# Two sandwich norms per sub-layer done in two token parts, between the last three and the first three weight tiles on either side

## The chip, the cores and the metric

The kernel runs on one NeuronCore of a Trainium2 chip. The metric is the device time of one execution in microseconds (us). The kernel before takes 1851.71 us (median of 3 runs, 1851.44 to 1854.57).

## The reference

Two layers over 512 latent tokens and 256 context tokens, with 1024 channels. What matters here is what stands between the big matrix products:

```python
for l in range(DEPTH):                              # DEPTH = 2
    u   = modulate(rms_norm(x, g_pre_mix[l]), sh1, sc1) @ w_in[l]      # latent tokens
    uc  = modulate(rms_norm(h_ctx, g_pre_mix[l]), csh1, csc1) @ w_in[l] # context tokens
    ...                                             # four head groups -> concatenated
    mix = jnp.concatenate([...], axis=-1) @ w_out[l]
    x = x + gt1 * rms_norm(mix, g_post_mix[l])
    ffn = swiglu(modulate(rms_norm(x, g_pre_ffn[l]), sh2, sc2), w_ffn_in[l], w_ffn_out[l])
    x = x + gt2 * rms_norm(ffn, g_post_ffn[l])
    if l < DEPTH - 1:
        ...                                         # the same two steps for h_ctx
```

`rms_norm` takes the mean of squares over the 1024 channels of a token. A norm after a product (post norm) therefore needs every output tile of the product, and the norm ahead of the next product (pre norm) needs all of the updated x.

## The kernel before, in words

**Layout.** Channels lie on the 128 partitions in 8 chunks, tokens on the free axis. Layer 0 works on 768 tokens (512 latent, then 256 context), layer 1 after its projections on the 512 latent ones. All matrix products are `L808`: a weight tile of 128 output channels is split into a high and a low part, and for each of its k chunks (8, or 6 in the last FFN group) there are three passes (high by high, high by low, low by high). A pass over 768 tokens is two matmuls of 384 columns, one over 512 tokens a single matmul of 512.

**The weight stream.** 196 tiles of 512 KB are read in order into a ring of 3 slots (`raw`, `w_hi`, `w_lo`). SyncE issues the load of tile k when the product of tile k-3 is done: `stream` waits on the semaphore `blk_done`. ScalarE then makes the high part (`L570`, `split_hi`) and VectorE the low part (`L1154`, `split_lo`), each at a place fixed in the engine's own program; so every engine runs its list in the order written.

**Between two groups of products** all is in one piece over all tokens. I call these places boundaries: B0 (output projection to FFN, layer 0, 768 tokens), B1 (FFN of layer 0 to the projections of layer 1, 768 tokens), B2 (output projection to FFN, layer 1, 512 tokens) and B3 (the end, 512 tokens, post norm and output only). At each one: the last tile is copied (ScalarE, `L579`) or added (VectorE, `L1181`) into `f_t`; GpSimd has summed the squares of tiles 0 to 6 (`L491`, `L493`); ScalarE squares the last tile (`L713`); TensorE sums over partitions with a matrix of ones (`L871`, float32); ScalarE makes the inverse root in two activations (`L708`, `L709`, `inverse_root`); VectorE scales and adds to x chunk by chunk (`post_norm`, `L1248`, `L1252`). Behind it ScalarE squares each chunk of x (`L702`), TensorE sums (`L859`), the root again, and then `pre_norm` makes the next product's input chunk by chunk: VectorE `tmp` (`L1226`), ScalarE `h_hi` (`L723`), VectorE `h_lo` (`L1233`). The first two tiles of the next group are multiplied side by side (`side_by_side`: chunk k into both banks as soon as it is there), and the third one after them.

**Names of tiles below.** At a boundary the eight output tiles before it are 0 to 7, and the tiles after it are 8, 9, 10, 11 and so on.

Of the kernel before, what the change touches and what calls it, by code (L numbers as in the profile page):

```python
# [20 lines left out]
F32 = mybir.dt.float32  # L21
# [4 lines left out]
D = 1024  # L26
# [48 lines left out]
HALF = TOK // 2  # L75

# [73 lines left out]
def hybrid_kernel(nc, xT, cvec, wstream, adaT, badaT, gT, rpb, wf, sink, lbT, hgT, dftL, dftC, dftD, rotm,  # L150
                  rope, swamask, namask, lvmask, sqc, out):
    with ExitStack() as ctx:
# [148 lines left out]
        x_upd, pn_m = sem("x_updated"), sem("post_norm_scaled")  # L301
        mix_done = sem("mixer_done")
# [104 lines left out]

        STEPS = [steps_after(l) for l in range(DEPTH)]
# [6 lines left out]
        def _(sp):  # L415
# [49 lines left out]
            for c in range(0, NC, 2):  # L465
                sp.wait_ge(x_upd, 2 * DEPTH * NC - NC + c + 2)
                sp.dma_start(outT[:, c:c + 2], x[:, c:c + 2, 0:LAT]).then_inc(s_out, 16)
            sp.wait_ge(s_out, 16 * NC // 2)
# [3 lines left out]
        def _(pool):  # L472
# [12 lines left out]

            def squares(g0, b0, n, T):

                for b in range(b0, min(b0 + n, N_OUT - 1)):
                    pool.wait_ge(bank_free[b % 2], g0 + b // 2 + 2)
                    f = f_t[:, b, 0:T]  # L490
                    link(pool.tensor_tensor(sq[:, 1 if b == 0 else 0, 0:T], f, f, ALU.mult))  # L491
                    if b:
                        link(pool.tensor_tensor(sq[:, 1, 0:T], sq[:, 1, 0:T], sq[:, 0, 0:T], ALU.add))  # L493
                    if b == N_OUT - 2:
                        pool.sem_inc(sq_sum, 1)
# [13 lines left out]
            for l in range(DEPTH):  # L509
# [38 lines left out]
                if l == 0:  # L548
                    ada_loads(11, 1)
                    squares(tp["wout"], 0, N_OUT, T)  # L550
                    ada_loads(12, 28)
                else:
                    squares(tp["wout"], 0, N_OUT, T)
                squares(tp["out", len(FFN_CHUNKS) - 1], 0, N_OUT, T)


        @block.scalar
        def _(act):
# [14 lines left out]
            def copy_phase(g0, n, dst, b0, T):  # L573

                for b in range(2 * n):
# [6 lines left out]
            def project(l, b):  # L582
# [5 lines left out]
                act.activation(as_product(u_t[:, blk, 0:T], T), product_of(ps[b % 2], T),  # L588
                               ACT.Silu if blk >= QD else ACT.Copy).then_inc(bank_free[b % 2], 1)

            def projections(l):
                g0 = 2 * TP[l]["proj"]
                for b in range(N_ALONE):
                    split_hi(g0 + b + 2)
# [82 lines left out]
            def splits_only(g0, n):  # L677

                for b in range(2 * n):
                    split_hi(2 * g0 + b + 2)  # L680

            def ffn_in(g0, n, T):
                for i in range(n):
                    k = 2 * (g0 + i)
                    split_hi(k + 2)
                    act.wait_ge(blk_done, k + 1)
                    act.wait_ge(bank_free[1], i + (g0 + 1))
                    act.activation(as_product(tmp[:, 0, 0:T], T), product_of(ps[0], T), ACT.Silu)\
# [22 lines left out]
            def late_mean_square(T):  # L711

                act.activation(lnms[:, 0:T], f_t[:, NC - 1, 0:T], ACT.Square).then_inc(sq_ready, 1)  # L713
                nsq[0] += 1
# [978 lines left out]
```

## Time and profile before

| | |
|---|---|
| median of 3 runs | 1851.71 us |
| profiled execution | 1851.98 us, of which the span from the first to the last instruction is 1850.2 us |
| chain that ended last, by engine | TensorE 85%, VectorE 9%, DMA 3%, ScalarE 2%, issue 1% |
| mean granted TensorE clock | 0.974 of full |
| TensorE busy | 1704.0 us (92% of the span) |
| VectorE, ScalarE, GpSimd busy | 980.6, 596.2, 149.1 us |

A busy TensorE is not one at its peak, since matmuls overlap in the records; the distance from one start to the next is what a matmul costs. "Idle before, releaser" is time in which the engine waited, and what ended the wait.

### The profile page before, as it was taken

The numbers are of one execution on the slowest core, as the hardware profiler recorded it, in microseconds if no ns is written. First come the engines' busy times: TensorE is split into PE (matmuls) and PEld (weight loads), VectorE is DVE, ScalarE is ACT, GpSimd is POOL, SyncE is SP. The second block draws the span as 40 slices with busy tenths as digits, with TensorE's granted clock in tenths as the row PEclk, the third lists the DMA queues.
The fourth block names the chain that finished last, engine by engine and source line by source line (L and its number), as shares of the span: only waits on it lengthen the run. The fifth ranks groups of instructions, "written<-read, shape, count | busy, mean of one in ns | idle before, by whom it ended". The sixth has DMA issues, their size and how long they took to land.

```text
span 1850.2 us, 24632 instructions
## 1 busy us (share of the span) xinstructions
PE 1704.0 (92%) x10460; PEld 1501.7 (81%) x10460; DVE 980.6 (53%) x1603; ACT 596.2 (32%) x796; POOL 149.1 (8%) x186
## 2 busy tenths in 40 slices
PE   2699998999799999999999979898899899999996
PEld 1699987769599999999999959796667587887874
DVE  7987536865566544555554372653762632233334
ACT  2334433732332222221122143542462422332231
POOL 1010001004100000000000400000103000000003
PEclk9899999999899999999999989999999899999998
DMA  8261124132133334333432202113402132232222
GB/s 335 88 204 48 47 63 105 50 114 84 54 103 116 124 125 135 116 126 125 128 113 91 69 23 69 58 47 83 112 34 69 46 102 91 91 102 91 91 92 102
DMA packets 80638, 178.84 MB, mean 97 GB/s; under 512 B 38912, under 2 KB 39424, under 8 KB 80272
## 3 DMA queue, kind: packets, MB, share of 16 engines
q1 hardware_dynamic: 66864, 122.70, 21.7%
q0 software_dynamic: 13664, 54.56, 8.6%
q8 instruction: 83, 1.36, 0.3%
q14 instruction: 27, 0.22, 0.0%
HBM read 175.14 MB, written 2.10 MB: 96 GB/s over the span
## 4 chain that ended last, share of the span: by engine, by line
PE 85%; DVE 9%; DMA 3%; ACT 2%; issue 1%; SPq 0%; DVEq 0%; ACTq 0%
PE psum L808 73%; PE psum L969 2%; PE psum L980 2%; PE psum L1003 2%; DMA ada_0a<-in_adaT 1%; DVE f_t L1248 1%; PE psum L1034 1%; DVE x L1252 1%; PE psum L859 1%; DVE tmp L1226 1%; PE psum L891 1%; DVE psum L1545 1%; DVE w_lo L1154 1%; DVE psum L1166 1%; DVE s_sb L1324 1%
## 5 line engine op out<-in xcount | busy, mean ns | idle before, releaser
L808 PE MATMUL psum<-h_hi,w_hi 128*128 128x384 f32 (+1 forms) x1872 | 560.4, 359 | 32.1 <-DVE h_lo L1233 27.3
L808 PE MATMUL psum<-h_lo,w_hi 128*128 128x384 f32 (+1 forms) x1872 | 547.5, 352 | 0.0
L808 PE MATMUL psum<-h_hi,w_lo 128*128 128x384 f32 (+1 forms) x1872 | 547.2, 352 | 0.0
L1154 DVE TENSOR_TENSOR w_lo<-raw,w_hi 128x1024 fp32r<-128x1024 f32 x194 | 241.2, 1243 | 352.2 <-ACT w_hi L570 350.9
L808 PEld LDWEIGHTS psum<-h_hi,w_hi 128*128 128x128 f32 x1872 | 342.7, 190 | 61.5 <-issue 34.7
L570 ACT ACTIVATE w_hi<-raw 128x1024 fp32r<-128x1024 f32 x194 | 205.6, 1060 | 501.3 <-DMA raw<-in_wstream 501.2
L808 PEld LDWEIGHTS psum<-h_lo,w_hi 128*128 128x128 f32 x1872 | 346.4, 190 | 20.6 <-issue 1.7
L808 PEld LDWEIGHTS psum<-h_hi,w_lo 128*128 128x128 f32 x1872 | 345.6, 190 | 19.9
L1166 DVE CUSTOM_DVE_ANT_0 psum<-ada_w,c_b 128x1024 f32<-128x1024 f32 x160 | 202.2, 1264 | 16.3 <-issue 3.7
L1194 DVE TENSOR_TENSOR tmp<-tmp,psum 128x768 f32<-128x768 f32 (+1 forms) x44 | 36.1, 821 | 263.6 <-PE psum L808 263.6
L808 PE MATMUL psum<-hid_hi,w_hi 128*128 128x384 f32 (+1 forms) x528 | 160.2, 357 | 15.6 <-DVE w_lo L1154 13.2
L808 PE MATMUL psum<-hid_lo,w_hi 128*128 128x384 f32 (+1 forms) x528 | 159.1, 355 | 0.0
L808 PE MATMUL psum<-hid_hi,w_lo 128*128 128x384 f32 (+1 forms) x528 | 159.0, 355 | 0.0
L808 PEld LDWEIGHTS psum<-hid_hi,w_hi 128*128 128x128 f32 x528 | 97.0, 189 | 27.1 <-DVE w_lo L1154 17.3
L808 PEld LDWEIGHTS psum<-hid_hi,w_lo 128*128 128x128 f32 x528 | 97.7, 190 | 7.0
L808 PEld LDWEIGHTS psum<-hid_lo,w_hi 128*128 128x128 f32 x528 | 97.8, 190 | 6.7
L859 PE MATMUL psum<-sq,consts 128*128 128x512 f32 (+1 forms) x112 | 50.0, 604 | 51.8 <-ACT sq L702 51.7
L477 POOL DMA_DIRECT2D ada_w<-in_adaT x78 | 41.3, 530 | 635.7 <-DVE ada_t L1166 635.1
L859 PEld LDWEIGHTS psum<-sq,consts 128*128 128x128 f32 x112 | 23.8, 226 | 77.5 <-issue 50.2
L491 POOL TENSOR_TENSOR sq<-f_t 128x768 f32<-128x768 f32 (+1 forms) x28 | 41.1, 1467 | 537.5 <-DVE f_t L1181 446.6
L692 ACT ACTIVATE hid_hi<-tmp 128x768 fp32r<-128x768 f32 (+1 forms) x44 | 32.5, 739 | 116.8 <-DVE tmp L1194 116.8
L588 ACT ACTIVATE u_t<-psum 128x768 f32<-128x768 f32 (+1 forms) x44 | 33.6, 763 | 100.7 <-PE psum L808 100.4
(168 smaller groups left out, 1453.9 us busy)
## 6 DMA issues: line engine op xcount, KB each, us to landing
raw<-in_wstream SPq DMA_DIRECT2D x196, 512.0 KB, 3.6
ada_w<-in_adaT POOLq DMA_DIRECT2D x80, 512.0 KB, 4.0
ada_0a<-in_adaT SPq DMA_DIRECT2D x6, 1024.0 KB, 14.3
x<-in_xT POOLq DMA_DIRECT2D x4, 1536.0 KB, 10.9
na_r<-in_rpb SPq DMA_DIRECT2D x64, 64.0 KB, 3.4
fn_l<-in_dftL POOLq DMA_DIRECT2D x2, 2048.0 KB, 8.2
ada_0b<-in_adaT SPq DMA_DIRECT2D x2, 1024.0 KB, 19.3
out_xT<-x SPq DMA_DIRECT2D x4, 512.0 KB, 2.8
```

The source lines that it names most:

```text
L477: pool.dma_start(ada_w[:, u], adaT[2 * ADA_ORDER[q] + (2 * ADA_FIRST + u)]).then_inc(ada_ld[u], 16)
L491: link(pool.tensor_tensor(sq[:, 1 if b == 0 else 0, 0:T], f, f, ALU.mult))
L570: act.activation(w_hi[:, k % RING].rearrange("p c n -> p (c n)"), raw[:, k % RING], ACT.Copy)\
L588: act.activation(as_product(u_t[:, blk, 0:T], T), product_of(ps[b % 2], T), ACT.Silu if blk >= QD else ACT.Copy).then_inc(bank_free[b % 2], 1)
L808: mm = pe.matmul(ps[u][:, at:at + hi - lo], w[:, slot, k], r[:, k, lo:hi], start=first, stop=last)
L859: mm = pe.matmul(ps[2][:, lo:hi], ones, sq[:, c % 2, lo:hi], start=c == 0, stop=c == NC - 1)
L969: mm = pe.matmul(dst, q, keys, start=True, stop=True)
L980: mm = pe.transpose(pt_ps[:, n * j + P * c:n * j + P * c + P], s_sb[:, v % 3, j, o:o + P], ident)
L1003: mm = pe.matmul(dst, val, pt_sb[:, v % 2, n * j + P * c:n * j + P * c + P], start=c == 0, stop=c == n // P - 1, skip_group_check=True)
L1154: dve.tensor_tensor(w_lo[:, k % RING].rearrange("p c n -> p (c n)"), raw[:, k % RING], w_hi[:, k % RING].rearrange("p c n -> p (c n)").bit ...
L1166: dve.tensor_tensor_reduce(ps[3][:], ada_w[:, u], c_b[:, v], 1.0, 0.0, ALU.mult, ALU.add, ada_t[:, u, v:v + 1]).then_inc(ada_done, 1)
L1194: dve.tensor_tensor(as_product(tmp[:, 1, 0:T], T), as_product(tmp[:, 0, 0:T], T), product_of(ps[1], T), ALU.mult).then_inc(bank_free[1], 1)
```

## The change

The norms at the four boundaries are done in two token parts. For 768 tokens part 0 is the 256 context tokens and part 1 the 512 latent ones; for 512 tokens the parts are halves of 256. The last three tiles of the product before (5, 6, 7) are multiplied first for part 0 and then for part 1 (`tail`), each into a bank of its own; the first three of the next product (8, 9, 10) first for part 0 and then, chunk by chunk and all three together, for part 1 (`head`). In `head` a part-1 pass over 768 tokens consists of matmuls of 384 and of 128 columns, beside the 256 of part 0. All three of its tiles report `blk_done` only in their last part-1 chunk. The mean squares are put inside these products on TensorE; VectorE and ScalarE get a written order (`norm_by_parts`) in which the weight splits of tiles 8, 9 and 10 stand between pieces of the norms. The gate products of layer 0 (`ada_pair`) start one step later in the FFN, and the output is stored in 8 pieces for 4.

```diff
+TAIL, HEAD = 3, 3
+def norm_parts(T):
+    return ((LAT, TOK, 1, 512), (0, LAT, 0, 0)) if T == TOK else ((0, T // 2, 0, 0), (T // 2, T, 0, 512))
...
+        def tail_bank(j):
+            return ps[(1, 0, 3)[j]]
+        def head_bank(j):
+            return ps[3] if j == HEAD - 1 else ps[j % 2]
...
 @block.gpsimd
+            def tail_squares(g0, T, nb):
+                for p, (lo, hi, _, _) in enumerate(norm_parts(T)):
+                    for j in range(TAIL - 1):
+                        b = N_OUT - TAIL + j
+                        if p == 0:
+                            pool.wait_ge(tail_free, TAIL * nb + j + 1)
+                        else:
+                            pool.wait_ge(bank_free[b % 2], g0 + b // 2 + 2)
+                        square(b, lo, hi)
+                    pool.sem_inc(sq_sum, 1)
...
 @block.scalar, the order at a boundary (norm_by_parts)
+                for j in range(TAIL):
+                    copied(0, j)
+                post_root(0)
+                pre_root(0)
+                copied(1, 0)
+                split_hi(2 * (g0 + N_OUT // 2))
+                normed_hi(0, 0, NC // 2)
+                copied(1, 1)
+                normed_hi(0, NC // 2, NC)
+                split_hi(2 * (g0 + N_OUT // 2) + 1)
+                copied(1, 2)
+                post_root(1)
+                split_hi(2 * (g0 + N_OUT // 2) + 2)
+                pre_root(1)
+                normed_hi(1, 0, NC)
...
 @block.tensor
+            def tail(g0, rhs_hi, rhs_lo, kc, T, nb, pre):
+                parts = norm_parts(T)
+                for p, (lo, hi, _, at0) in enumerate(parts):
+                    for j in range(TAIL):
+                        b = N_OUT - TAIL + j
+                        if p == 0:
+                            pe.wait_ge(w_lo_done, 2 * g0 + b + 1)
...
+                        for k in range(kc):
+                            mm = passes_into(tail_bank(j), 2 * g0 + b, k, rhs_hi, rhs_lo, ((lo, hi, at0),), k == 0, k == kc - 1)
+                            if k == kc - 1:
+                                mm.then_inc(blk_done if p else tail_done, 1)
+                            if p and j == 0 and k == 2:
+                                late_mean_square(parts[0])
+                            if p and j == 1 and pre:
+                                part_mean_square(parts[0], NC * k // kc, NC * (k + 1) // kc)
+            def head(g0, T, nb):
+                for j in range(HEAD):
+                    pe.wait_ge(w_lo_done, 2 * g0 + j + 1)
+                    for k in range(NC):
+                        if j == 0:
+                            pe.wait_ge(hlo_ready, base + k + 1)
+                        passes_into(head_bank(j), 2 * g0 + j, k, h_hi, h_lo, head_pieces(T, 0), k == 0, k == NC - 1)
+                        if j == 0 and k == 3:
+                            late_mean_square(parts[1])
+                part_mean_square(parts[1], 0, NC)
+                for u in range(2):
+                    pe.wait_ge(bank_free[u], g0 + 1)
+                for k in range(NC):
+                    pe.wait_ge(hlo_ready, base + NC + k + 1)
+                    for j in range(HEAD):
+                        mm = passes_into(head_bank(j), 2 * g0 + j, k, h_hi, h_lo, head_pieces(T, 1), k == 0, k == NC - 1)
+                        if k == NC - 1:
+                            mm.then_inc(blk_done, 1)
...
 @block.vector, the order at a boundary (norm_by_parts)
+                for j in range(TAIL):
+                    added(0, j)
+                root()
+                post(0, 0, NC)
+                dve.wait_ge(x_upd, nx[0])
+                added(1, 0)
+                if pre is None:
+                    added(1, 1)
+                    added(1, 2)
+                    root()
+                    post(1, 0, NC)
+                    dve.wait_ge(x_upd, nx[0])
+                    return
+                root()
+                normed(0, 0, NC // 2)
+                split_lo(nxt)
+                added(1, 1)
+                normed(0, NC // 2, NC)
+                split_lo(nxt + 1)
+                added(1, 2)
+                root()
+                post(1, 0, 2)
+                split_lo(nxt + 2)
+                post(1, 2, NC)
+                dve.wait_ge(x_upd, nx[0])
+                root()
+                normed(1, 0, NC)
```

`post(p, c0, c1)` is the post norm and `normed(p, c0, c1)` the pre norm of part p for chunks c0 to c1; `nxt` is tile 8.

## Rows read from the trace of the kernel before

**Rows 1.** Who waited for whom: total us, times, longest.

```profile
PE psum L859 <- ACT sq L702: 51.7, 7, 34.5
PE psum L808 <- DVE h_lo L1233: 27.3, 4, 12.7
```

**Rows 2.** VectorE, SyncE and ScalarE in order of time around B1.

```profile
1069.16 0.95 DVE L1181 TENSOR_TENSOR f_t<-f_t,psum 128x768 f32<-128x768 f32 x1 [0.24 <-PE psum L808]
...
1116.58 18.20 SPq L429 DMA_DIRECT2D raw<-in_wstream  x4
...
1121.19 1.23 DVE L1154 TENSOR_TENSOR w_lo<-raw,w_hi 128x1024 fp32r<-128x1024 f32 x1 [7.13 <-ACT w_hi L570]
...
1126.13 0.81 ACT L588 ACTIVATE u_t<-psum 128x768 f32<-128x768 f32 x1 [2.60 <-PE psum L808]
```

**Rows 3.** ScalarE and VectorE at B0 (two rows), then at B2 (two rows).

```profile
477.21 0.81 ACT L579 ACTIVATE f_t<-psum 128x768 f32<-128x768 f32 x1 [3.73 <-PE psum L808]
...
533.19 0.81 ACT L688 ACTIVATE tmp<-psum 128x768 f32<-128x768 f32 x1 [3.05 <-PE psum L808]
...
1440.23 0.60 ACT L579 ACTIVATE f_t<-psum 128x512 f32<-128x512 f32 x1 [0.87 <-PE psum L808]
...
1484.80 0.69 DVE L1194 TENSOR_TENSOR tmp<-tmp,psum 128x512 f32<-128x512 f32 x1 [3.64 <-PE psum L808]
```

**Rows 4.** The chain: products of 384 and then 512 columns without a wait.

```profile
643.66 200.16 PE psum L808 x1152
...
1563.37 119.98 PE psum L808 x528
```

**Rows 5.** TensorE in order of time: float32 matmuls of 256 and 512 columns.

```profile
379.40 5.63 PE L883 MATMUL psum<-fn_d,u_t 128*128 128x256 f32 x24
385.72 7.13 PE L891 MATMUL psum<-fn_l,fn_ab 128*128 128x512 f32 x16 [0.69 <-ACT fn_ab L778]
```

**Rows 6.** Groups by form: float32 of 128 columns; weight loads of 128 and 64.

```profile
L1082 PE MATMUL psum<-hv,hk 128*128 128x128 f32 x80 | 10.2, 275 | 0.0
...
L808 PEld LDWEIGHTS psum<-h_lo,w_hi 128*128 128x128 f32 x1872 | 346.4, 190 | 20.6 <-issue 1.7
...
L1034 PEld LDWEIGHTS psum<-hq,hs 64*64 64x64 f32 x1120 | 20.0, 137 | 11.1 <-issue 11.1
```

**Rows 7.** The chain at B1: post norm of one chunk, 768 tokens.

```profile
1077.64 1.06 DVE f_t L1248 x2
1078.70 0.87 DVE x L1252
```

**Rows 8.** The chain at B3: last add, root, post norm, 512 tokens.

```profile
1832.72 0.70 DVE f_t L1181
...
1835.34 0.70 ACT lnms L708
...
1836.06 0.64 ACT rstd L709
...
1838.81 0.66 DVE f_t L1248
1839.47 0.60 DVE x L1252
...
1845.79 1.20 DVE x L1252 x2
```

**Rows 9.** ScalarE group by form: h_hi of 256 columns.

```profile
L723 ACT ACTIVATE h_hi<-tmp,col_sh 128x256 fp32r<-128x256 f32 x24 | 11.8, 494 | 0.0
```

**Rows 10.** GpSimd shortly before B2: squares of 512 columns.

```profile
1435.53 1.04 POOL L491 TENSOR_TENSOR sq<-f_t 128x512 f32<-128x512 f32 x1 [3.03 <-ACT f_t L579]
1436.65 1.29 POOL L493 TENSOR_TENSOR sq<-sq 128x512 f32<-128x512 f32 x1
```

**Rows 11.** TensorE at B1, just after the products start again.

```profile
1099.09 0.84 PE L808 MATMUL psum<-h_lo,w_hi 128*128 128x384 f32 x2
1099.73 0.84 PE L808 MATMUL psum<-h_hi,w_lo 128*128 128x384 f32 x2
```

More of the change, by code:

```diff
@@ L802, in passes, with passes_into @@
             def passes(tile, k, rhs_hi, rhs_lo, T, begin, end):
-                u, slot = tile % 2, tile % RING
+                return passes_into(ps[tile % 2], tile, k, rhs_hi, rhs_lo, pieces(T), begin, end)
+            def passes_into(bank, tile, k, rhs_hi, rhs_lo, tokens, begin, end):
+                slot = tile % RING
                 for w, r, first, last in ((w_hi, rhs_hi, begin, False), (w_hi, rhs_lo, False, False),
                                           (w_lo, rhs_hi, False, end)):
-                    for lo, hi, at in pieces(T):
-                        mm = pe.matmul(ps[u][:, at:at + hi - lo], w[:, slot, k], r[:, k, lo:hi], start=first, stop=last)
@@ L1170, in ada_pair, with lo_phase @@
                 dve.tensor_copy(dst, ada_t[:].rearrange("p u v -> p (u v)")).then_inc(ada_copied, 1)
[L1172 removed]
+            def lo_phase(g0, n, ada=(0, 0), add=False, T=TOK, tail=0):
                 for i in range(n):
@@ L1236, in pre_norm, with norm_by_parts, added, root @@
                 dve.wait_ge(hlo_ready, nlo[0])
-            def post_norm(l, gt, g, T):
-                cols(l, gt, col_gg)
-                link(dve.tensor_tensor(col_gg[:], col_gg[:], gain(l, g), ALU.mult))
-                nrs[0] += 1
-                dve.wait_ge(rstd_ready, nrs[0])
-                st = STREAMS[:2 if T == TOK else 1]
-                for c in range(NC + 1):
-                    if c < NC:
-                        for lo, hi, v in st:
+            def norm_by_parts(l, gt, g_post, sh, sc, g_pre, T, g0, nb, add, pre):
+                parts = norm_parts(T)
+                def added(p, j):
+                    if not add:
+                        return
+                    b = N_OUT - TAIL + j
+                    lo, hi, _, at0 = parts[p]
+                    if p == 0:
+                        dve.wait_ge(tail_done, TAIL * nb + j + 1)
+                    else:
+                        dve.wait_ge(blk_done, 2 * g0 + b + 1)
+                    dst = f_t[:, b, lo:hi]
+                    dve.tensor_tensor(dst, dst, tail_bank(j)[:, at0:at0 + hi - lo], ALU.add)\
+                       .then_inc(bank_free[b % 2] if p else tail_free, 1)
+                def root():
+                    nrs[0] += 1
+                    dve.wait_ge(rstd_ready, nrs[0])
+                def post(p, c0, c1):
+                    lo, hi, v, _ = parts[p]
+                    for c in range(c0, c1 + 1):
+                        if c < c1:
@@ new lines, in norm_by_parts @@
+                nxt = 2 * (g0 + N_OUT // 2)
+                cols(l, gt, col_gg)
+                link(dve.tensor_tensor(col_gg[:], col_gg[:], gain(l, g_post), ALU.mult))
+                if pre is not None:
+                    cols(pre, sh, col_sh)
+                    cols(pre, sc, col_sc)
+                    link(dve.scalar_tensor_tensor(col_gs[:], col_sc[:], 1.0, gain(pre, g_pre), ALU.add, ALU.mult))
+                for j in range(TAIL):
+                    added(0, j)
+                root()
```

243 lines of the change are left out of this document (167 added, 76 removed).

## The prediction, on record before the change was run

> **What bounds the kernel now.** I read the page first: TensorE carries 85% of the chain that ended last. The waits then show where it stands still: 51.7 us until ScalarE has squares of x (34.5 of them before the first product, which the change leaves alone) and 27.3 us until VectorE has the first `h_lo` of a product [rows 1]. Both stand at the boundaries. The engines in order of time give what a boundary costs from the start of tile 5 to the start of tile 11, the stretch that the change rewrites. Tile 7 of B1 is done at 1069.13 [rows 2]. A pass of 384 columns takes 200.16 / 1152 = 0.174 us and one of 512 takes 119.98 / 528 = 0.227 us [rows 4], so a tile over 768 tokens takes 8.34 us with 8 chunks and 6.25 us with 6, and over 512 tokens 5.45 and 4.09. Tile 5 of B1 therefore started at 1050.4; tile 10 is done at 1126.1 [rows 2]: **B1 is 75.7 us** long. In the same way **B0** is 533.2 - (477.2 - 25.0) = **81.0** and **B2** is (1484.8 - 5.45) - (1440.2 - 16.35) = **55.5**, since that last row marks tile 11's end [rows 3]. **B3** runs from tile 5 to the end of the span: 1850.2 - (1832.7 - 12.3) = **29.8** [rows 8].
>
> **What stays equal and what is added on TensorE.** Over 768 tokens the tail's parts have the same columns and the same number of matmuls. The head's passes become three matmuls (256, 384, 128) for two. No product (`L808`) of 256 or 128 columns is in the trace. The fixed part of a matmul is 0.174 - 0.160 = 0.014 us, so 256 columns take about 0.12 (0.107 of streaming). For 128 columns there are two bounds: 0.067 by the same sum, and 0.127, the distance of float32 matmuls with 128 columns and a full weight load each (10.2 / 80, [rows 6]). I take 0.12, near the upper one, because the weight load seems to bind: its record is 190 ns for 128 columns of weights and 137 ns for 64 [rows 6], 53 ns more for 64 columns, so a full load occupies some 107 ns, and it is done anew for every matmul. Part 1 of the head then takes 24 x 3 x (0.174 + 0.12) = 21.2 us, part 0 takes 8.6, together 29.8 for 25.0 before: 4.8 us more at B0 and at B1. The Trainium skill ("TensorE: Matmul & The Clock Gate", Back-to-back issue gap) gives columns over 2.4 GHz plus 2.5 ns, about 56 ns for 128 columns; by that B0 and B1 would each be some 4.6 us shorter than I sum. This trace's 14 ns of fixed cost speaks against the 2.5. Over 512 tokens each matmul of 512 becomes two of 256: 0.24 for 0.227.
>
> The mean squares now stand in TensorE's own program. One float32 instruction leaves two records, and records of 256 and 512 columns stand some 0.23 and 0.44 us apart (5.63 / 24 and 7.13 / 16, each a little less because the last one drains), so 256 columns cost 0.46 and 512 cost 0.88 us [rows 5].
>
> **VectorE and ScalarE by parts.** From the two widths [rows 7, 8]: scaling 0.66 for 512 columns and 1.06 - 0.66 = 0.40 for 256; the add 0.60, and by its slope of 0.27 per 256 columns 0.33. So post norm costs 0.73 us a chunk for 256 tokens and 1.26 for 512. A pre-norm chunk of 256 is two scalings and a completion, 0.91; its first `h_lo` needs `tmp`, `h_hi` (0.49 [rows 9]) and `h_lo` in turn, 1.5. Root: 1.36 for 512 [rows 8], 0.96 for 256 (two activations near the 0.49).
>
> **B1, step by step** (t = 0 at the start of tile 5).
> 1. Tile 7's weights are loaded when tile 4 is done, at 0. Load 3.5, `split_hi` 1.1, `split_lo` 1.2: the low part comes 5.84 us after the issue even where nothing is in the way (1121.19 + 1.23 - 1116.58 [rows 2]). Tiles 5 and 6 of part 0 take only 2 x 2.16, so TensorE idles until 6.0; part 0 ends at 8.1.
> 2. Add and square of part 0, its float32 sums behind the third chunk of tile 5 (GpSimd's squares of 256, some 1.4 us a tile from [rows 10], are ready by 10.3), root: 12.4. Post norm 8 x 0.73: 18.3.
> 3. The mean square of part 0 is spread over tile 6, which ends with it at 21.3; root: 22.5. Tile 7 ends at 25.4.
> 4. VectorE could begin the pre norm at 22.5, but ScalarE first does `split_hi` of tile 8 (1.1). Four chunks end at 27.0, and only then comes `split_lo` of tile 8: 28.2. TensorE, done at 25.4, idles 2.9.
> 5. VectorE adds tile 6 (0.6), norms the other four chunks (to 32.7), waits for `split_hi` of tile 9, splits (34.5), adds tile 7 (35.1). Square 0.63: 35.9. TensorE stands in the middle of tile 8, behind the wait for that square, since 29.7: 5.3 us idle there, less one sum.
> 6. Root: 38.4. Post norm of two chunks, `split_lo` of tile 10 (42.1), six more chunks: 49.7. TensorE does the head's part 0 until 45.1 and the eight sums of part 1 until 52.2. Root, `tmp`, `h_hi`, `h_lo`: 56.2, so 4.0 us idle.
> 7. Part 1 of the head: 21.2, to 77.4.
> 8. Tile 11 cannot be loaded before tile 8 is done. Before, tiles 8 and 9 finished together and tile 10 (8.3 us) covered the load. Now all three finish within 1.8 us of the end: 77.4 - 1.8 + 5.84 and some 0.2 of waits is **81.7**, so TensorE idles 4.4.
>
> The serial chain of VectorE and ScalarE has not become shorter; both parts' norms are in one line, and the splits stand in it too.
>
> **The clock.** Where products start again after a boundary the rows show the lower level, 1.2 for 2.4 GHz: pairs of matmuls of 384 columns start 0.64 us apart in place of 0.35 [rows 11]; I put the loss at 1.7 us a start, an estimate for the ten pairs or fewer that I read at that distance at B0 and B1. Before, each boundary pays that once, and the lengths above hold it. Now part 1 of the head starts after 4.0 us idle and tile 11 after 4.4; with 0.2 for the stop in tile 8 I add 3.5: B1 is 85.2, **9.5 more**.
>
> **B0** has two chunks more a tile: part 0 ends at 8.9, tile 7 at 29.9; ScalarE copies where VectorE added. First `h_lo` of part 1 at 58.0, end of the head 79.2, tile 11 at 83.5, with the clock 87.0: **6.0 more**.
>
> **B2**, parts of 256: part 0 ends at 8.9, its sums 20.1, tile 7 at 23.0, `split_lo` of tile 8 27.3 (4.5 idle), square of part 1 32.8 (3.5 idle), first `h_lo` 47.8 (2.8 idle), head 24 x 3 x 0.12 = 8.6 to 56.5. The reload covers less, since two passes of a chunk are only 0.72: 61.9; with the clock 65.4: **9.9 more**.
>
> **B3**: part 0 is ready at 8.1, post norm from 11.8 to 17.7. The tail ends at 16.0, but VectorE adds part 1 only from 17.8, and GpSimd needs until 21.2 for two tiles. Sums and root: 23.4, post norm 29.2, and 3.2 for the last store as before (the last adds end at 1847.0 [rows 8], the span at 1850.2): 32.4, **2.6 more**. Eight stores in place of four lie beside the post norm.
>
> Elsewhere nothing on the path changes; the gate products start a step later and are still done before B1. Sum: 6.0 + 9.5 + 9.9 + 2.6 = 28.0. The profiled execution took 1851.98 us, 0.3 above the median, so I predict **1880 us**.
>
> **Rivals.**
> A. *Small matmuls stream at their columns.* With 0.067 for 128 columns B0 and B1 each lose 3.8 less: 1872. For it the linear fixed cost; against it the weight record. Chance 0.20.
> B. *Weight load is the whole price.* If a matmul cannot start its load until the one before has streamed, each small one takes the record's 0.19 [rows 6]. Summed in the same way B0 and B1 grow by 12.6 and 9.8, B2 by 16.2, B3 by about 5: 1924. Against it: float32 loads of the same size follow each other at 0.127. Chance 0.04.
> C. *The cover works, and it is faster.* Decided by step 5: the pre norm of part 0 must be through by the time the tail ends (25.4 at B1, against my 32.7). It would be if VectorE and ScalarE passed the splits and waits of steps 4 and 5 without holding TensorE. Then the chain of part 1 starts at the end of the tail, and with steps 6 to 8 unchanged B1 ends near 73, B0 and B2 3 us under before, B3 equal: 9 us gained, 1843. For it: 25 us of products now lie beside the norms. Against it: the order of VectorE's program. Chance 0.11.
> D. *No net change*, the losses of the reload and the small matmuls just cancelling such a gain. Chance 0.04.
> My own case keeps 0.61.
>
> **How the numbers follow.** A difference under 0.2% (3.7 us) can't be told from none. Slower is my case, A and B: 0.85; faster is C, 0.11; same is D, 0.04. Low end: case A with no second clock loss (3 x 1.6) and 5 us of shorter waits, 1862. High end: a reload slowed by the three loads issued at once (some 1.8 us at three places) and clock losses also in the head's part 0 (2 us at three places), 1892. Outside lie B, C and D, 0.19 together.
>
> **What would show it.** Right: no product for 4 to 5 us behind the head at three places, ended by `w_lo` of tile 11; two stops of 3 to 5 us inside the first head tile; first head product waiting for `w_lo` of tile 8; matmuls of 128 columns 0.12 apart from the next; the boundaries at 87, 85, 65 and 32. Wrong: head products that start with no wait behind the tail, or tile 11 ready at once.

## The result, and the profile after

The changed kernel takes **1898.11 us** (median of 4 runs, 1897.41 to 1902.14), the kernel before 1851.59 beside it (4 runs): a ratio of 1.0242, interval [1.0222, 1.0262]. It is 46.5 us slower, where 28 us were forecast and 1892 was the high end. Direction and most of the mechanism were right; the size was not, and two terms were missing.

The waits of TensorE after (who waited for whom, total us, times, longest), to be read against [rows 1]:

```profile
PE psum L909 <- DVE w_lo L1325: 48.9, 19, 5.4
PE psum L1019 <- ACT sq L743: 34.0, 1, 34.0
PE psum L909 <- DVE h_lo L1407: 12.7, 1, 12.7
PE psum L909 <- DVE h_lo L1459: 10.6, 3, 3.9
PE psum L1031 <- ACT lnms L783: 9.6, 3, 4.7
PE psum L1031 <- POOLq L531: 5.9, 3, 5.1
```

Of the 51.7 us for squares of x only the 34.0 before the first product are left: the pre norms' sums no longer hold TensorE. In their place stand the low parts of weight tiles (`w_lo`, 48.9 us in 19 waits, where the kernel before has 17.9 in 8), the first `h_lo` of part 1 (three waits of up to 3.9), and the late sum, which waits for ScalarE's square of tile 7 (`lnms`) and for GpSimd.

TensorE in order of time at B1 after (start, duration, line, operands, count; in brackets the idle time before and what ended it): the first product of tile 5, the second half of the late sum of part 1 with two products behind it, the first products of the head's part 1 and later ones, and tile 11:

```profile
1062.44 0.28 PE L909 MATMUL psum<-hid_hi,w_hi 128*128 128x256 f32 x1
...
1099.69 2.08 PE L1031 MATMUL psum<-lnms,consts 128*128 128x512 f32 x2 [4.68 <-ACT lnms L783]
...
1101.78 0.41 PE L909 MATMUL psum<-h_lo,w_hi 128*128 128x256 f32 x1
1101.99 0.41 PE L909 MATMUL psum<-h_hi,w_lo 128*128 128x256 f32 x1
...
1121.78 0.77 PE L909 MATMUL psum<-h_hi,w_hi 128*128 128x384 f32 x2 [3.93 <-DVE h_lo L1459]
1122.35 0.73 PE L909 MATMUL psum<-h_lo,w_hi 128*128 128x384 f32 x2
1122.88 0.73 PE L909 MATMUL psum<-h_hi,w_lo 128*128 128x384 f32 x2
...
1128.44 0.45 PE L909 MATMUL psum<-h_lo,w_hi 128*128 128x384 f32 x2
1128.73 0.45 PE L909 MATMUL psum<-h_hi,w_lo 128*128 128x384 f32 x2
...
1149.91 1.01 PE L909 MATMUL psum<-h_hi,w_hi 128*128 128x384 f32 x2 [4.40 <-DVE w_lo L1325]
1150.72 0.84 PE L909 MATMUL psum<-h_lo,w_hi 128*128 128x384 f32 x2
...
1155.98 0.51 PE L909 MATMUL psum<-h_lo,w_hi 128*128 128x384 f32 x2
1156.32 0.51 PE L909 MATMUL psum<-h_hi,w_lo 128*128 128x384 f32 x2
```

Tile 5 starts at 1062.4 and tile 11 at 1149.9: B1 is 87.5 us long, where it was 75.7. The distances between starts tell the clock. In the head a pair of 384 and 128 columns comes every 0.53 us from 1122.35, and every 0.29 us from 1128.44; behind tile 11's wait the pairs of two times 384 come every 0.64 us, and every 0.34 to 0.35 from 1155.98. Each of the two waits leaves TensorE at the lower of its two levels (1.2 for 2.4 GHz; the granted clock is 0.51 and 0.50 there) for 5 to 6 us, which costs 11 x 0.25 = 2.7 and 8 x 0.29 = 2.4 us. Behind the late sum it is the same: twelve products of 256 columns from 1101.78 on start 0.21 us apart in place of 0.12, another 1.1 us.

The pair also settles the disputed price: 0.287 less 0.174 for 384 columns [rows 4] is 0.113 us for 128 columns, near the 0.12 that I took.

The boundaries after, and the clock there (busy time of each engine in each stretch, number of instructions, then PEclk, the granted clock as a share of 2.4 GHz):

```profile
450.00:545.00 95.00, 77.98 (x416) 66.26 (x416) 56.45 (x83) 36.49 (x60) 19.43 (x14) 0.91 0.16 50
1065.00:1160.00 95.00, 77.39 (x388) 65.79 (x388) 48.76 (x82) 32.51 (x52) 9.54 (x10) 0.87 0.11 35
1455.00:1530.00 75.00, 59.12 (x351) 52.22 (x349) 41.41 (x81) 32.49 (x62) 7.20 (x8) 0.89 0.15 50
```

From the starts of tiles 5 and 11 (B0: 451.4 and 542.9; B2: 1451.0 and 1515.4; B3: 1862.5 and the end of the span, 1895.6), read to some 0.2 us, with the forecast as it stood without the 1.6 us behind tile 11's start:

| | before | after | more | forecast, without the clock behind tile 11 |
|---|---|---|---|---|
| B0 | 81.0 | 91.5 | 10.5 | 4.4 |
| B1 | 75.7 | 87.5 | 11.8 | 7.9 |
| B2 | 55.5 | 64.4 | 8.9 | 8.3 |
| B3 | 29.8 | 33.1 | 3.3 | 2.6 |
| everything else | | | 10.9 | 4.8 |

The sum is the 45.4 us between the two spans (1850.2 and 1895.6), "everything else" being the remainder.

### The profile page after: what moved, and what is told of

Same layout as the page of the kernel before. It is cut to its first block, busy times and chain, and to the rows that moved or that the text cites. A ratio compares the mean times of both kernels' runs of the same rounds, so it can differ in the third digit from the quotient of the medians.

```text
span 1895.6 us, 25550 instructions
## 1 busy us (share of the span) xinstructions
PE 1730.1 (91%) x10826; PEld 1532.8 (81%) x10826; DVE 998.7 (53%) x1673; ACT 606.7 (32%) x852; POOL 156.5 (8%) x202
## 4 chain that ended last, share of the span: by engine, by line
PE 81%; DVE 10%; DMA 4%; ACT 3%; issue 1%; POOL 0%; SPq 0%; DVEq 0%; ACTq 0%; POOLq 0%
PE psum L909 68%; PE psum L1138 2%; PE psum L1149 2%; DMA raw<-in_wstream 2%; PE psum L1172 2%; DVE w_lo L1325 1%; PE psum L1040 1%; DMA ada_0a<-in_adaT 1%; DVE psum L1337 1%; PE psum L1203 1%; ACT w_hi L609 1%; PE psum L1060 1%; DVE s_sb L1565 1%; DVE tmp L1453 1%; DVE psum L1787 1%
## 5 line engine op out<-in xcount | busy, mean ns | idle before, releaser
L909 PE MATMUL psum<-h_hi,w_hi 128*128 128x384 f32 (+3 forms) x1968 | 595.3, 357 | 56.6 <-DVE w_lo L1325 33.2
L909 PE MATMUL psum<-h_lo,w_hi 128*128 128x384 f32 (+3 forms) x1968 | 576.2, 347 | 0.0
L909 PE MATMUL psum<-h_hi,w_lo 128*128 128x384 f32 (+3 forms) x1968 | 575.3, 347 | 0.0
L909 PEld LDWEIGHTS psum<-h_hi,w_hi 128*128 128x128 f32 x1968 | 364.1, 193 | 88.6 <-DVE w_lo L1325 36.4
L1337 DVE CUSTOM_DVE_ANT_0 psum<-ada_w,c_b 128x1024 f32<-128x1024 f32 x160 | 202.3, 1264 | 11.6 <-DMA ada_w<-in_adaT 3.2
L909 PE MATMUL psum<-hid_hi,w_hi 128*128 128x384 f32 (+2 forms) x546 | 169.7, 358 | 18.6 <-DVE w_lo L1325 15.8
L909 PE MATMUL psum<-hid_lo,w_hi 128*128 128x384 f32 (+2 forms) x546 | 166.5, 352 | 0.0
L909 PE MATMUL psum<-hid_hi,w_lo 128*128 128x384 f32 (+2 forms) x546 | 166.1, 351 | 0.0
L510 POOL TENSOR_TENSOR sq<-f_t 128x512 f32<-128x512 f32 (+2 forms) x36 | 45.8, 1272 | 567.2 <-DVE f_t L1354 422.8
L729 ACT ACTIVATE tmp<-psum 128x768 f32<-128x768 f32 (+1 forms) x44 | 31.1, 706 | 102.9 <-PE psum L909 102.9
L851 ACT ACTIVATE s_sb<-s_sb,nb 128x512 f32<-128x512 f32 (+3 forms) x80 | 56.8, 713 | 7.8 <-DVE nb L1569 6.5
## 6 DMA issues: line engine op xcount, KB each, us to landing
x<-in_xT POOLq DMA_DIRECT2D x4, 1536.0 KB, 10.9
```

What stands on the lines that cost most here:

```text
L510: link(pool.tensor_tensor(sq[:, 1 if b == 0 else 0, lo:hi], f, f, ALU.mult))
L851: act.activation(p, p, ACT.Exp, bias=nb[:, s % 3, j:j + 1], scale=SCALE, accum_out=sums[:, s % 3, j:j + 1]).then_inc(at_p, 1)
L909: mm = pe.matmul(bank[:, at:at + hi - lo], w[:, slot, k], r[:, k, lo:hi], start=first, stop=last)
L1337: dve.tensor_tensor_reduce(ps[3][:], ada_w[:, u], c_b[:, v], 1.0, 0.0, ALU.mult, ALU.add, ada_t[:, u, v:v + 1]).then_inc(ada_done, 1)
```

## The experiments

All ratios are to the kernel before, run beside each; the changed kernel stands at 1898.1 and 1.0242.

| run | median us | ratio, interval |
|---|---|---|
| e1_reload | 1878.3 | 1.0137 [1.0113, 1.0162] |
| e2_contig | 1887.1 | 1.0184 [1.0160, 1.0208] |
| e3_splits | 1889.9 | 1.0202 [1.0184, 1.0221] |
| e4_gates | 1895.2 | 1.0227 [1.0210, 1.0245] |
| e5_busy | 1885.9 | 1.0180 [1.0155, 1.0204] |
| e6_no_squares | 1891.2 | 1.0205 [1.0187, 1.0223] |
| e7_end_whole | 1892.9 | 1.0212 [1.0189, 1.0235] |
| e8_together | 1859.6 | 1.0036 [1.0026, 1.0046] |
| e9_sum_later | 1868.1 | 1.0079 [1.0055, 1.0103] |
| e10_later_busy | 1872.6 | 1.0103 [1.0083, 1.0123] |
| e11_before_busy | 1848.3 | 0.9973 [0.9960, 0.9986] |
| e12_together_busy | 1853.3 | 1.0005 [0.9996, 1.0014] |

### The reload behind the head

```diff
-                    for j in range(HEAD):
+                    for j in range(HEAD - 1):
                         mm = passes_into(head_bank(j), 2 * g0 + j, k, ...)
...
+                for k in range(NC):
+                    mm = passes_into(head_bank(HEAD - 1), 2 * g0 + HEAD - 1, k, h_hi, h_lo, head_pieces(T, 1), ...)
+                mm.then_inc(blk_done, 1)
```

Part 1 of tiles 8 and 9 goes chunk by chunk, tile 10 follows whole, so that its products cover the load of tile 11.

> The changed kernel, but in the head's part 1 only tiles 8 and 9 go chunk by chunk together; tile 10's part 1 comes after them as a whole. Same matmuls, other order. My theory: tile 11 is late because tile 8 is done only at the end of the head, 6.1 us before tile 11 can start. Then tile 10 (24 x 0.287 = 6.9 us over 768 tokens, 24 x 0.12 = 2.9 over 512) covers the reload: the wait before tile 11 falls from 4.3 to about 0 at B0 and B1 and from 5.4 to about 2.5 at B2, and the half rate behind it (2.5 us a place) goes with it at B0 and B1: 1898 - 2 x 6.8 - 3 = about 1881. Rival: the load is not what is late, VectorE's order behind the head is: no change, 1898.

Measured: 1878.3, 20 us less. The `w_lo` wait before tile 11 is gone at B0 and B1, and 2.8 us long at B2:

```profile
PE psum L909 <- DVE w_lo L1329: 37.3, 16, 5.1
```

48.9 us in 19 waits have become 37.3 in 16, so 11.6 us of waiting are gone. The other 8 us of the gain have to come from what stood behind the waits. Step 8 of the forecast is confirmed, and of the edits tried it gives back the most.

### The price of the small matmuls

```diff
-                    return ((0, HALF, 0), (HALF, LAT, 512)) if p else ((LAT, TOK, 512 + LAT - HALF),)
+                    return ((0, LAT, 0),) if p else ((LAT, TOK, 512),)
```

The head's tiles lie contiguously in their bank, so part 1 is one matmul of 512 columns in place of 384 and 128; the readers of the three tiles are changed to match.

> The changed kernel, but over 768 tokens the three head tiles hold their tokens in one piece in the bank, so that a part-1 pass is one matmul of 512 columns and not 384 and 128. If a matmul of 128 columns costs its weight load (0.287 us for the pair after the change, against 0.227 for one of 512), 72 passes save 0.06 each at B0 and B1: 8.6 us, 1889. If it costs only its columns and 0.014 (0.241 for the pair), 2 us, 1896.

Measured: 1887.1, 11 us less. 0.227 [rows 4] for 0.287 over 72 pairs is 4.3 us at each of B0 and B1; the other 2 us fit the same passes at half rate, which start 0.43 us apart in this run's trace for 0.53 (some ten passes at each place). The rival that small matmuls stream at their columns (A) is out.

### The splits out of the chain

```diff
                 root()
                 normed(0, 0, NC // 2)
-                split_lo(nxt)
                 added(1, 1)
                 normed(0, NC // 2, NC)
-                split_lo(nxt + 1)
                 added(1, 2)
+                split_lo(nxt + 1)
+                split_lo(nxt + 2)
                 root()
-                post(1, 0, 2)
-                split_lo(nxt + 2)
-                post(1, 2, NC)
+                post(1, 0, NC)
```

`split_lo(nxt)` goes ahead of the first `root()`, and ScalarE's `split_hi` are moved in the same way, into stretches where both engines wait for sums.

> The changed kernel, but the weight splits of tiles 8, 9 and 10 stand in both engines where they wait for a root: tile 8 ahead of the pre norm of part 0, tiles 9 and 10 ahead of the post norm of part 1. The same instructions. My theory, that the serial chain of VectorE and ScalarE holds TensorE: 2.3 us less ahead of tile 8, 1.7 at tile 9, up to 1.2 at tile 10, some 5 us at each of B0, B1 and B2: about 1883. Rival: the chain is not what binds, and the time moves under 3 us: 1895 to 1898.

Measured: 1889.9, 8 us less, half of what was expected. At B1 of this run the post norm of part 1 ends at 1109.3, but TensorE is in the head's part 0 until 1106.5 and in the eight sums until 1114.3. The chain of VectorE and ScalarE, shortened, runs into TensorE's own order of work. So the shortened chain no longer sets the first `h_lo` of part 1; that this is the whole of the missing half is argued, not measured.

### The gate products at B0

```diff
+                if l == 0:
+                    ada_pair(10)
+                    ada_pair(11)
                 for i in range(N_OUT // 2):
...
-                    if l == 0 and i < 2:
-                        ada_pair(10 + i)
```

After the change the gate products 10 and 11 meet the tail of B0. VectorE there, and GpSimd beside it, in the changed kernel:

```profile
449.46 2.21 DVE L1337 CUSTOM_DVE_ANT_0 psum<-ada_w,c_b 128x1024 f32<-128x1024 f32 x1
...
451.75 2.70 DVE L1337 CUSTOM_DVE_ANT_0 psum<-ada_w,c_b 128x1024 f32<-128x1024 f32 x1
...
455.71 3.99 DVE L1325 TENSOR_TENSOR w_lo<-raw,w_hi 128x1024 fp32r<-128x1024 f32 x2
```

```profile
450.65 2.71 POOL L512 TENSOR_TENSOR sq<-sq 128x768 f32<-128x768 f32 x1
453.44 2.33 POOL L510 TENSOR_TENSOR sq<-f_t 128x768 f32<-128x768 f32 x1
455.85 2.77 POOL L512 TENSOR_TENSOR sq<-sq 128x768 f32<-128x768 f32 x1
```

The two `w_lo` take 3.99 us for 2 x 1.23 [rows 2], and tile 6 stands 2.57 us for its low part (`456.98`, ended by `w_lo`).

> The changed kernel, but the two gate products that VectorE does between the weight splits of the output projection of layer 0 stand before them, in its 15 us of waiting. If they are why tile 6 waits 2.6 us for its low part at B0, that wait goes and the time falls by 2.6 us, to 1895.5; if the load is late as well, it stays near 1898.

Measured: 1895.2, an interval that overlaps the changed kernel's. By the trace tile 6 no longer waits (tile 7 waits 0.47 us) and B0 becomes 2.0 us shorter (454.8 to 544.35, 89.5 for 91.5), but tile 5 starts 3.4 us later: more than B0 gains is paid ahead of it instead. So the delay is real, and whether this edit wins any of it back can't be told from these runs.

### The clock behind the waits

```diff
+            def keep_busy(n, at):
+                for _ in range(n):
+                    pe.matmul(ps[2][:, at:at + P], ones, ident, start=True, stop=True)
...
                 part_mean_square(parts[1], 0, NC)
+                keep_busy(10, 896 if T == TOK else 384)
                 for u in range(2):
                     pe.wait_ge(bank_free[u], g0 + 1)
...
+                keep_busy(13, 896 if T == TOK else 384)
```

> TensorE gets work that nobody reads, in the two waits of each head: 10 float32 products of 128 columns before it waits for the first h_lo of part 1, and 13 before tile 11, into PSUM columns that no one uses; nothing else is changed. At some 0.25 us each (two records of 0.127) they take 2.5 and 3.3 us of waits of 3 to 4 us, so they don't delay anything. Theory (the granted clock is down to half behind each stall and costs 2.5 to 2.7 us there): tile 11 at B0, B1 and B2 and the first chunks of part 1 run at full rate, 3 x 2.6 for tile 11 and up to 3 x 1 for part 1, so 1898.1 falls to 1888 to 1890.5. Rival (the clock is down for another reason, or such work doesn't keep it up): unchanged, 1898, or up to 6 us more where the products themselves run at half rate and overshoot the wait.

Measured: 1885.9, 12 us less. That is somewhat more than the theory's 8 to 10, which the interval (1.0155 to 1.0204, or 1881 to 1890) does not exclude. TensorE at the same place of B1: the first pair of the head's part 1, the 13 idle products (26 records) and tile 11:

```profile
1118.87 0.47 PE L909 MATMUL psum<-h_hi,w_hi 128*128 128x384 f32 x2 [1.70 <-DVE h_lo L1465]
...
1120.62 0.45 PE L909 MATMUL psum<-h_hi,w_hi 128*128 128x384 f32 x2
1120.91 0.45 PE L909 MATMUL psum<-h_lo,w_hi 128*128 128x384 f32 x2
...
1139.54 3.12 PE L946 MATMUL psum<-consts 128*128 128x128 f32 x26
1144.11 0.62 PE L909 MATMUL psum<-h_hi,w_hi 128*128 128x384 f32 x2 [1.46 <-DVE w_lo L1331]
1144.57 0.51 PE L909 MATMUL psum<-h_lo,w_hi 128*128 128x384 f32 x2
1144.92 0.52 PE L909 MATMUL psum<-h_hi,w_lo 128*128 128x384 f32 x2
```

Both places run at the upper level from the first pair (0.29 and 0.35 us apart), although TensorE waits as long for real work as before. B0 looks the same. At B2 the filling left 2.42 us idle before tile 11, and its products fell to half rate all the same (0.43 us apart from 1505.47, for 3.5 us in place of 5.2). The loss is the clock's, and it depends on what TensorE does in the wait.

### GpSimd beside VectorE

```diff
-                        square(b, lo, hi)
+                        if p == 0:
+                            square(b, lo, hi)
```

> GpSimd leaves out the squares of tiles 5 and 6 over part 1, so they are missing from the mean squares of part 1 (the values change, no other instruction does). Theory (GpSimd's squares slow VectorE's pre norm of part 0 by some 1.3 us at B1, and as much at B0 and B2, and hold the last sum of B3): 3 x 1.3 at B0 to B2, and at B3 the wait of 5.1 us shortens by about 2.9; with some 0.5 us a boundary for sums that come before the clock falls, 1898.1 falls to 1890 to 1891. Rival (VectorE's longer operations have nothing to do with GpSimd): only B3's part goes, 1895.

Measured: 1891.2, 7 us less, as the theory had it. This kernel leaves the squares of tiles 5 and 6 over part 1 out of the mean squares. At B3 the wait for GpSimd falls from 5.09 to 2.43 us; the rest of the gain lies ahead of B3. VectorE at B1 in the changed kernel, and GpSimd at that time:

```profile
1090.99 1.66 DVE L1453 SCALAR_TENSOR_TENSOR tmp<-x,col_gs,rstd 128x256 f32<-128x256 f32 x2
1092.57 1.49 DVE L1459 SCALAR_TENSOR_TENSOR h_lo<-tmp,col_sh,h_hi 128x256 fp32r<-128x256 f32 x1
```

```profile
1091.22 1.15 POOL L510 TENSOR_TENSOR sq<-f_t 128x512 f32<-128x512 f32 x1 [7.19 <-DVE f_t L1427]
1092.44 1.34 POOL L512 TENSOR_TENSOR sq<-sq 128x512 f32<-128x512 f32 x1
```

The same three operations without GpSimd:

```profile
1088.45 0.87 DVE L1454 SCALAR_TENSOR_TENSOR tmp<-x,col_gs,rstd 128x256 f32<-128x256 f32 x2
1089.50 0.49 DVE L1460 SCALAR_TENSOR_TENSOR h_lo<-tmp,col_sh,h_hi 128x256 fp32r<-128x256 f32 x1 [0.18 <-ACT h_hi L803]
```

0.79 and 1.00 us of VectorE's time were GpSimd's. At B0 of the changed kernel the same operations meet squares as well, and there 0.9 and 1.8 us are lost (1.40 us at 481.74 for 0.48, and this pair, which takes 0.88 us elsewhere):

```profile
486.37 2.68 DVE L1453 SCALAR_TENSOR_TENSOR tmp<-x,col_gs,rstd 128x256 f32<-128x256 f32 x2
```

In the Trainium skill ("SBUF — State Buffer", SBUF: two separate sides) VectorE operations with two SBUF inputs and GpSimd operations share a pair of ports under an exclusive lock, and the loser is blocked for the whole instruction; the trace agrees (0.49 becomes 1.49 beside a GpSimd operation of 1.34, and ends 0.28 us after it).

### The end as before

```diff
-                tail(tp["out", len(FFN_CHUNKS) - 1], hid_hi, hid_lo, FFN_CHUNKS[-1], T, 2 * l + 1, full[l])
-                if not full[l]:
-                    late_mean_square(norm_parts(T)[1])
+                if full[l]:
+                    tail(tp["out", len(FFN_CHUNKS) - 1], hid_hi, hid_lo, FFN_CHUNKS[-1], T, 2 * l + 1, full[l])
+                else:
+                    late_mean_square((0, T, 0, 0))
...
```

> The end of the program (B3) is done as in the kernel before: the last three tiles over all 512 tokens, one late mean square, one post norm and four stores; B0 to B2 stay by parts. Theory (parts only cost at B3: 33.1 for 29.8): 3.3 us less, 1894.8. Rival (B3 is longer only because of what stands ahead of it): unchanged, 1898.1.

Measured: 1892.9, 5 us less than the changed kernel, with an interval (1.0189 to 1.0235) that holds the forecast's 3.3 and reaches that kernel's own. By the trace tile 5 of B3 starts 29.7 us before the end of the span, where it was 33.1. Parts cost at B3 and bring nothing, since no head stands behind them.

### All edits, and TensorE's order

The edits of e1 to e4 and of e7 together:

> The four edits of the first experiments together (reload, contiguous head tiles, splits early, gate products early) and the end as before. Theory (separate losses, so they add): 1898.1 - 20 - 11 - 8 - 3 - 3.3 = 1853, the kernel before within the error. Rival (they overlap: with the splits early TensorE itself, not VectorE's chain, sets the start of part 1's head, so shorter head tiles gain there again, and the sum is exceeded by 3 to 5 us: 1848 to 1850). Second rival (each fills the same stall, so that less than the sum comes back): 1860 or more.

Measured: 1859.6, 0.4 us short of the second rival's 1860: 38.5 us come back, 7 less than the sum. TensorE at B1 of this run: two stops in tile 8 and one before part 1.

```profile
1080.05 2.07 PE L1053 MATMUL psum<-sq,consts 128*128 128x512 f32 x2 [2.85 <-POOLq L530]
1084.29 2.08 PE L1053 MATMUL psum<-lnms,consts 128*128 128x512 f32 x2 [2.17 <-ACT lnms L792]
...
1106.43 0.76 PE L927 MATMUL psum<-h_hi,w_hi 128*128 128x512 f32 x1 [3.93 <-DVE h_lo L1501]
```

The next edit puts the late sum behind tile 9:

```diff
-                        if j == 0 and k == 3:
+                        if j == 1 and k == NC - 1:
                             late_mean_square(parts[1])
```

> As the five edits together (1859.6), and TensorE does the late sum of part 1 (which waits for the square of tile 7) after the head's tile 9 over part 0, no longer behind the fourth chunk of tile 8. Theory: in those five edits' run TensorE stands 4.6 us at B0 and 5.0 at B1 in the middle of tile 8 with 4.3 us of part 0's products queued behind the wait, and its own order (part 0's tiles, then the eight sums) then sets the start of part 1; with these products ahead of the wait the stop shrinks to under 1 us and up to 4 us a boundary come back: 1859.6 - 6 to 10 = 1850 to 1854. Rival (VectorE's chain sets the start of part 1 anyway, and a later sum only delays its root): 1860 to 1863.

Measured: 1868.1, 8.5 us more: my theory fell, and its rival fell short of the size. Counted from tile 6's start, which is 4.2 us later in this run, the late sum's second half now comes at 37.1 us in place of 28.7, since tile 9 has a wait of its own, with the sum behind it:

```profile
1090.65 0.58 PE L927 MATMUL psum<-h_hi,w_hi 128*128 128x256 f32 x1 [2.64 <-DVE w_lo L1348]
...
1095.94 1.11 PE L1053 MATMUL psum<-sq,consts 128*128 128x512 f32 x2
```

VectorE splits tile 9 only behind the pre norm of part 0 and the add of tile 7, so the chain square, sum, root, post norm waited for a tile that it does not need. Part 1 of the head starts 5.0 us later for it (55.8 us after tile 6 for 50.8).

> As the run with the later sum, and in each head 9 float32 products of 128 columns that nobody reads before the wait for the first h_lo of part 1, and 9 before tile 11. Theory (behind each of these waits the clock is at half for some 5 us, which costs 2.6): 6 places, of which some 4 still fall to half: 6 to 12 us less than the run with the later sum, 1840 to 1847, faster than the kernel before. Rival (after waits of under 3 us the clock hardly falls): within 2 us of the run with the later sum.

Measured: 1872.6, 4.5 us more than the run before, with overlapping intervals: no gain, and the theory's 6 to 12 are excluded. At B1 the products fell to half rate again 1.5 us behind the 9 idle ones (0.43 apart from 1118.87 for 0.23 at 1117.23). Whether a longer filling would have held, I did not try there.

### Keeping TensorE busy, on both sides

The kernel before, with 16 idle products between the pre norm's sums and the products, at B0 to B2:

```diff
                 mean_square(TOK)
+                if l:
+                    keep_busy(16)
                 projections(l, chunks_split(2))
...
                 mean_square(T)
+                keep_busy(16)
                 ready = chunks_split(2 if full[l] else 1)
```

> The kernel before, and at B0, B1 and B2 16 float32 products of 128 columns that nobody reads, between the eight sums of the pre norm and the wait for the first h_lo. Theory (the clock is at half behind the 5.3 us of waiting, eight pairs 0.29 us longer each): 3 x 2.3 less, 1852 - 5 to 7 = 1845 to 1847. Rival (VectorE's h_lo, not TensorE's rate, paces the first chunks of a phase): within 2 us of the kernel before.

Measured: 1848.3, ratio 0.9973 [0.9960, 0.9986]: faster than both kernels, by the 5 us that were the theory's low end. At B1 TensorE stands 1.76 us for the first `h_lo`, where it stood 5.33, and the pairs start 0.35 us apart at once, where [rows 11] has 0.64:

```profile
1092.26 3.73 PE L813 MATMUL psum<-consts 128*128 128x128 f32 x32
1097.76 0.59 PE L808 MATMUL psum<-h_hi,w_hi 128*128 128x384 f32 x2 [1.76 <-DVE h_lo L1240]
1098.18 0.52 PE L808 MATMUL psum<-h_lo,w_hi 128*128 128x384 f32 x2
1098.54 0.52 PE L808 MATMUL psum<-h_hi,w_lo 128*128 128x384 f32 x2
```

At B0 and B2 of this run the half rate is gone as well.

And the five edits, with the late sum in its old place and all waits of the head filled (`keep_busy` as above stands before part 1 and before tile 11, and the line below fills the late sum's two waits):

```diff
-                            late_mean_square(parts[1])
+                            late_mean_square(parts[1], (6 if T == TOK else 2, 7))
```

> The five edits together (1859.6), the late sum of part 1 back in its place inside tile 8, and float32 products of 128 columns that nobody reads in all waits of a head: 6 (2 at B2) before the late sum, 7 before the square of tile 7, 9 before the first h_lo of part 1 and 9 before tile 11. Theory (each of these stops leaves the clock at half behind it: the last sum 2.08 for 1.1 us at B0 and B1, then 13 to 18 matmuls of 256 columns at 0.21 for 0.12, about ten pairs or matmuls more before tile 11 and in part 1): 3 to 5 us a boundary, 1859.6 - 9 to 14 = 1845 to 1851, level with the kernel before or just under it, and not under 1844. Rival (VectorE's and ScalarE's chain paces these stretches, so that TensorE's rate in them buys next to nothing): 1856 to 1860, above the kernel before.

Measured: 1853.3 beside 1853.3 of the kernel before, 1.0005 [0.9996, 1.0014]; 6 us less than the five edits alone, between the theory's 9 and the rival's 3.6. The clock is what the filling restored. From the start of tile 5 to the start of tile 11 the granted clock is 1.00, 0.98 and 1.00 at B0, B1 and B2, where the changed kernel has 0.91, 0.89 and 0.91 in the same stretches:

```profile
453.10:529.60 76.50, 72.31 (x391) 58.16 (x390) 48.77 (x77) 36.30 (x59) 12.86 (x12) 1.00 0.18 57
1047.00:1121.90 74.90, 67.77 (x357) 54.14 (x355) 48.83 (x83) 31.50 (x51) 10.81 (x10) 0.98 0.15 44
1419.10:1478.80 59.70, 53.95 (x385) 48.65 (x383) 36.82 (x77) 29.64 (x58) 8.80 (x10) 1.00 0.19 62
```

With the waits filled on both sides the norms by parts at B0 to B2 are 5 to 6 us slower than the whole norms (1853.3 against 1848.3, ratios 1.0005 and 0.9973), so over the three boundaries the form of the change gains nothing here. The stretches show that this is not so at each of them. Beside the kernel before, B0 takes 76.4 us for 81.0 and B1 74.9 for 75.7, but B2, which has 512 tokens, takes 59.6 for 55.5; beside the whole norms with filled waits (80.4, 74.3 and 54.3 by the same marks in e11_before_busy) B0 gains 4 us (1 us of it is paid ahead, where tile 5 starts later), B1 is even and B2 loses 5. These are readings of one execution each. A kernel with parts at B0 alone was not run.

## Why the prediction was right in kind and short in size

**Right.** The stops at B1 came where the steps put them: before tile 8 (2.58 us for 2.9), inside it (4.68 for 5.3 less one sum), before part 1 (3.93 for 4.0) and before tile 11 (4.40 for 4.4). The low part of tile 7, the root and post norm of part 0 and the first four `h_lo` of B1 were each met within 0.4 us. The reload took 6.08 us for 6.04, from tile 8's end (1143.83) to tile 11's start. Small matmuls cost 0.113 and 0.119 us for 0.12 and 0.12. Rivals A, B, C and D are out: A by e2_contig, B by 0.113 for 0.19, C and D by the result. One of the signs named for being right was not seen: inside tile 8 there is one stop of 3 to 5 us at B0 and B1 (3.11 and 4.68) and none at B2 (1.85), not two. The 56 ns against which the 0.12 was weighed are the figure for a matmul alone (see the last section).

**The step that failed is the clock's**, as a size: "I put the loss at 1.7 us a start [...] I add 3.5", with 0.2 us of it for the stop in tile 8. Measured at B1 are 2.7 us in part 1 of the head and 2.4 behind tile 11, and at the stop in tile 8 not 0.2 but some 2: the late sum of part 1 runs at half rate (2.08 us at 1099.69; 1.12 where e12_together_busy keeps the clock up), and so do the twelve products behind it (1.1 us), and the chain waits for both. So 3.5 should have been about 7 at B1; at B0 it was about 6 and at B2 about 4. In the kernel before eight pairs run at the distance of [rows 11] at B1 (8 x 0.29 = 2.3 us) but five at B0 (506.23 to 509.56, 1.5 us), so 1.7 was fair for what it was read from; the spells after the change are longer.

Part of it lies outside the boundaries. Behind tile 11 some 2.4 us are lost at each of B0, B1 and B2 for 1.6, which is 2.5 of the 6.1 us that "everything else" is over. Another 3.3 us stand between B2 and B3, where the wait of 2.07 us for `w_lo` that both kernels have at three places is followed by full rate at all three before, and by a spell of half rate at two of them after (1592.50 and 1837.84). The first of them in the two kernels, 11.2 us long, with 48 products in one and 42 in the other:

```profile
1552.11:1563.30 11.19, 11.16 (x48) 8.90 (x48) 1.62 (x2) 1.66 (x2) 0.00 (x0) 1.00 0.07 29
```

```profile
1590.94:1602.10 11.16, 11.16 (x42) 9.05 (x43) 1.61 (x2) 1.06 (x1) 0.00 (x0) 0.85 0.08 29
```

Why such a wait lets the clock fall at one place and not at another stays open. Nothing near them is changed, and which of them are followed by half rate differs from run to run (of the same three, none in e12_together_busy, one in e11_before_busy, two in e8_together), so these 3.3 us may belong to the profiled execution and not to the change. e5_busy, which takes away two spells a boundary, shows that the clock's share is some 12 us, give or take 6.

**Two terms were missing.** GpSimd beside VectorE was counted as nothing. It cost VectorE's chain 1.8 us at B1 and 2.7 at B0, and leaving the squares out gained about 7 us in all (e6_no_squares), of which 2.7 are B3's wait for GpSimd, which was in the forecast. And "Elsewhere nothing on the path changes; the gate products start a step later" was wrong: with the tail's parts the low parts of tiles 6 and 7 are due 4 us sooner, the gates and GpSimd's squares stand in their way, and B0 pays 2.6 us.

These terms fall ahead of part 1 of the head. Its first product came 64.1 us after tile 5's start at B0 for 58.0, 59.3 for 56.2 at B1 and 48.7 for 47.8 at B2, and from there to tile 11 all three went within 0.7 us of the forecast, where by luck the cheaper pair (0.287 us for 0.294) offsets part of the longer spell of half rate. Together, as an estimate from these readings, the clock has some 10 of the 17.4 us between the forecast and the two spans, GpSimd beside VectorE up to 4.5 and the gates 2.6.

**Where the gain went.** At B0 and B1 some 25 us of products do lie beside the norms now. Over the whole kernel the edits give back 20 us for the reload behind the head with its clock, 11 for the split matmuls and 8 for the splits in the chain, and the filled waits another 6. With all of this mended TensorE's fixed order (tiles 9 and 10 of part 0, then the eight sums) ends later than the post norm of part 1 (B1 of e3_splits) and so sets when part 1 can start.

## What to carry to other kernels

Before work is split to cover a serial chain, list what each piece makes late: the slot of a ring that comes free later, the matmul that becomes two, the wait that stands in an in-order queue ahead of products that could go. Price each stop of TensorE at its idle time plus the half-rate spell behind it, read from the same trace, and try first to fill the stop with products that nobody reads; here that alone was worth 5 us on the old kernel, more than all the restructuring. Judge a cover boundary by boundary: here it gained at one of four. Where a late sum sits in an engine's queue, place it by the arrival of its input and not by how much work could go ahead of it.

## What the runs showed of the hardware

- After a stop of 3.9 to 4.4 us at B0 and B1 of the changed kernel TensorE ran at half rate for 5 to 6 us (granted clock 0.50 to 0.52). With the stop filled with float32 products down to 1.4 to 1.8 us idle it ran at full rate from the first matmul (e5_busy at B0 and B1, e11_before_busy). With 1.9 us left the clock fell 1.2 to 1.5 us behind the stop at B1 of e10_later_busy and of e12_together_busy, and not at B0 of e12_together_busy; with 2.4 us left it fell (tile 11 at B2 of e5_busy). An unfilled stop of 2.07 us was followed by either, and so was one of 2.34 (full rate from 643.66, half from 847.26 in the kernel before).
- A product of 128 columns costs 0.113 us and one of 256 0.119: below 256 columns a matmul with a weight load of its own gains next to nothing. The Trainium skill ("TensorE: Matmul & The Clock Gate", Back-to-back issue gap) has 56 ns for a matmul of 128 columns alone and about 81 ns in a stream with a weight load before each; for these products the trace agrees with neither, and the measurement decides.
- VectorE's gate products, 1.26 us each in the mean over the kernel before, took 2.2 to 2.7 us beside GpSimd's squares of 768 columns, and those took 2.3 to 2.8 us for 1.47 and 1.85 at B1 (1063.73 and 1065.28 in the changed kernel), where no gate product runs. So both sides lose.
